# Prompt attention of a hybrid decoder step: queries, keys and values stored by head, weighing on two column halves, sums of probabilities on GpSimd

## The chip, the cores and the metric

The kernel runs on one core of a Trainium2 chip. The metric is the device time of one execution in microseconds; the time before is the median of three runs.

## The reference

One inference step of a two-layer decoder trunk for a prompt of 2048 tokens and eight samples of eight new tokens each, all in fp32. The part that the change touches is the forgetting attention of the prompt in the even layer, with 8 heads of 64:

```python
def fox_prompt(q, k, v, logf):              # blocks of 128 queries
    cum = jnp.cumsum(logf, axis=1)
    s = einsum('bqhd,bkhd->bhqk', qi, k) * D ** -0.5
    s = s + ci[..., None] - cum_t[:, :, None, :]
    s = where(qpos >= kpos, s, NEG_INF)
    p = softmax(s, axis=-1)
    return einsum('bhqk,bkhd->bqhd', p, v)
```

Before it stand a normalisation and the projection `z = u @ w_in`, which yields q, k and v (k and v are outputs of the step too) and the operands of retention. Behind it come retention, a gated output projection, an RG-LRU layer and a last norm. The samples attend to 8192 cached tokens each, in pages of 128.

## The kernel before

The kernel is written in phases, with engines that meet at semaphores. Each phase ends with a barrier of all engines.

`in_proj` runs twice over 17 token tiles of 128 rows (16 of the prompt, one of the samples). Half 0 makes q, k, v of the attention and rq, half 1 the rest. A tile's four groups of 512 columns are three fp32r matmuls for each of 8 slices (lines 125 to 127), evacuated by ScalarE or VectorE into one buffer `z` per group, and stored by SP as rows of 2 KB to `fq`, `fk`, `fv`, `rq` (line 525).

`attention` handles head t of the prompt and, interleaved, batch t of the samples' cached pages. TensorE, VectorE, ScalarE, GpSimd and SP all walk one list of events, made by `merge` from the prompt's list (`fox_events`) and the samples' (`samp_events`); each engine has handlers for the kinds that concern it. `merge` takes from whichever list has spent the smaller share of its planned cost, and puts an event of the other list ahead if a look would follow a look by less than 0.85 of planned cost. So every planned cost moves the order.

The prompt's 16 key tiles and 4 groups of 512 queries give 40 steps a head (4, 8, 12 and 16). At a step:
- a *look* (lines 1633, 1634) writes scores of a later query block to bank `ps_n`; VectorE masks it where it lies on the diagonal and takes its row maximum (line 1461). The next look waits for that maximum.
- a *score* (1651, 1652) writes transposed scores [keys, queries], with the maximum already taken off, to one of two banks `ps_k`; the diagonal is masked on VectorE (1480).
- *exp* (1368): ScalarE writes the probabilities to one of four buffers `prob`. Tiles on the diagonal have only 384, 256 or 128 of the 512 queries.
- a *weigh* (1667), two steps behind: one fp32 matmul with v as stationary operand. v has a 65th column of ones, so that row 64 of `ps_o` collects the sums of probabilities.

After a group's last weigh comes *keep* (ScalarE copies `ps_o` to `o_t`, 1373), and three steps into the next group *out*: four transposes of `o_t` into bank `ps_x` (1674), from which VectorE divides by the sum (1486, 1490). `ps_x` also serves the transposes of the next head's q and k (1684) and the turned maxima (1641), one at a time.

Of the samples, *s_turn* is VectorE's transpose of gathered keys (1512), after which GpSimd gathers the next group of pages (1293); *s_score* (1692, 1698) and *s_weigh* (1724) are fp32 matmuls in tiles of 32 columns of the array, four side by side. SP loads the V pages (1220), and at a head's end the natural q, k and v of the head after next (1230, 1231): 2048 pieces of 256 B for each of the three, out of token-major rows. GpSimd further copies the high parts of q and k (1320, 1322). `retention` has a product in two column halves (2119): `ps_o[half * HD:(half + 1) * HD, a, :]`.

Of the kernel before, what the change touches and what calls it, by code (L numbers as in the profile page):

```python
# [32 lines left out]
P = 128  # L33
D = 1024
# [320 lines left out]
class AttentionTables:  # L355


    def __init__(self, ph, io):
# [6 lines left out]
        self.causal = ph.sb("causal", [P, NS])  # L365
        self.own = ph.sb("own_half", [P, 2, HD])
# [12 lines left out]
    def load(self, sp):  # L379
        for dst, name in [(self.ident, "identity"), (self.mask, "causal_bias"), (self.mask_t, "causal_bias_t")]:  # L380
            sp.dma_start(dst[:, :], self.io[name]).then_inc(self.consts_in, 16)
# [21 lines left out]
def in_proj(nc, io, half):  # L403


    with ExitStack() as ctx:
# [4 lines left out]
        dests = [io["fq"], io["fk"], io["fv"], io["rq"]] if first else [io["rk"], io["rv"], io["g0"], io["g1"]]  # L411
# [3 lines left out]
        GN = 4  # L415

# [69 lines left out]
        def _(sp):  # L486
            for s in u_stored + z_stored:
                sp.sem_inc(s, 16)
            if first:
# [24 lines left out]
            def step(t, i, par):  # L514
# [19 lines left out]
            for g in range(GN):  # L534
                sp.wait_ge(z_stored[g], 16 * (T + 1))
# [13 lines left out]
        def _(act):  # L549
# [16 lines left out]
            def step(t, i, par):  # L566
# [3 lines left out]
                for g in by_act:  # L570
# [5 lines left out]
                    else:  # L576
                        act.wait_ge(z_stored[g], 16 * (t + 1))
# [27 lines left out]
        def _(dve):  # L605
# [35 lines left out]
            def step(t, i, par):  # L641
# [3 lines left out]
                for g in range(GN):  # L645
                    if g == rot:
                        rotary(t, i, par)
                    elif g in gated:
                        dve.wait_ge(*evac[g].at(t))
                        if g == 2:  # L650
                            dve.wait_ge(z_stored[g], 16 * (t + 1))
# [4 lines left out]
                    elif g not in by_act:  # L656
                        dve.wait_ge(*z_done.at(t, g))
                        dve.wait_ge(z_stored[g], 16 * (t + 1))
# [207 lines left out]
def attention(nc, io, tables):  # L866
# [5 lines left out]
    with ExitStack() as ctx:  # L872
# [25 lines left out]
        def fox_events(last):  # L898
# [3 lines left out]
            for s in range(steps + 2):  # L902
# [136 lines left out]
        v = ph.sb("fox_v_one", [P, 2, PT, HD + 1])  # L1039
# [4 lines left out]
        o_t = ph.sb("fox_o_t", [HD + 1, G])  # L1044
# [64 lines left out]
        ones_set = ph.sem("ones_set")  # L1109
# [11 lines left out]
        weighed = ph.count("weighed", steps, 4)  # L1121
        o_copied = ph.count("o_copied", GQ)
# [52 lines left out]

        def x_free(t, u):
# [33 lines left out]
        def _(sp):  # L1210
            sp.sem_inc(stored, 16)
            for n, name in enumerate(["fq", "fk"]):
                sp.dma_start(nat_s[:, n, :], io[name][LAST, 0:ROWS, :]).then_inc(s_consts_in, 16)
# [14 lines left out]
            def fetch(t, par, rows_ready=()):  # L1228
                for n, name in enumerate(["fq", "fk"]):
                    sp.dma_start(nat[:, n], io[name][0:PT, :, bass.ds(t * HD, HD)].rearrange("t p d -> p t d")).then_inc(head_in, 16)  # L1230
                sp.dma_start(v[:, par, :, 0:HD], io["fv"][0:PT, :, bass.ds(t * HD, HD)].rearrange("t p d -> p t d")).then_inc(v_in[par], 16)
# [1929 lines left out]
```

## Time and profile before

| | |
|---|---|
| three runs | 3680.77, 3687.21, 3688.68 us; median 3687.21 |
| profiled execution | 3679.39 us, span 3677.7 |
| busy | TensorE 3280.4, weight loads 2492.7, VectorE 1721.9, ScalarE 1282.1, GpSimd 296.6 |
| mean granted TensorE clock | 0.94 |
| DMA | 360931 packets, 627.36 MB, 118185 of them under 512 B |
| projection, half 0 and half 1 | to about 440, to about 850 us |
| attention | from about 917 to 1976 us |

Times are of one execution, in microseconds from the start of its span. PE is TensorE's matmuls and PEld its weight loads, DVE is VectorE, ACT ScalarE and POOL GpSimd. A matmul's record includes the latency of its tail, so that records overlap; the distance from start to start tells what one costs in a stream. An fp32 matmul leaves two load records and two matmul records; a transpose, and an fp32r matmul, one of each. A shape such as 128*65 gives the rows and columns of the array that an instruction uses.

### The profile page before, as it was taken

The page shows a single profiled execution, that of the slowest core. Times are in us where ns is not written, and L with a number is a line of the kernel's source. Part 1 is how long each engine was busy: PE and PEld are TensorE (multiplying, and loading weights), DVE is VectorE, ACT ScalarE, POOL GpSimd, SP SyncE. Part 2 cuts the span into 40 slices and gives each one's busy share as a digit, 9 for nine tenths or more (in the row PEclk, how much of TensorE's full clock was granted, in tenths as well). Part 3 has the DMA queues.
Part 4 walks back from the last instruction along what each step waited for, and adds up shares of the span by engine and source line. Part 5 has one row for each costly group of instructions (what it writes and reads, how often), then busy time and mean ns, then how long its engine had stood idle before and what let it go on. Part 6 is the DMA issues. An engine that isn't in the chain of part 4 may idle for free. (4 is left out here: it accounts for less than half of the span.)

```text
span 3677.7 us, 63038 instructions
## 1 busy us (share of the span) xinstructions
PE 3280.4 (89%) x22374; PEld 2492.7 (68%) x22374; DVE 1721.9 (47%) x2974; ACT 1282.1 (35%) x2326; POOL 296.6 (8%) x306
## 2 busy tenths in 40 slices
PE   6999789995799899999996859999869999499998
PEld 5888678884465565556554757888747777378887
DVE  3222221242676666667652744333346676443333
ACT  3111121211134334334433533333356666533232
POOL 0000000111211111111100530000000000000000
PEclk9999899996599999999998979999979999699999
DMA  5333442344688888888866863333244433332221
GB/s 140 116 116 115 173 133 96 107 142 124 214 300 285 265 317 281 272 281 312 293 207 204 291 237 121 113 117 127 94 174 138 129 129 109 114 119 91 79 90 59
DMA packets 360931, 627.36 MB, mean 171 GB/s; under 512 B 118185, under 2 KB 180689, under 8 KB 344274
## 3 DMA queue, kind: packets, MB, share of 16 engines
q1 hardware_dynamic: 341410, 487.62, 39.6%
q0 software_dynamic: 19264, 136.46, 10.6%
q8 instruction: 144, 2.36, 0.3%
q14 instruction: 113, 0.93, 0.1%
HBM read 488.74 MB, written 135.22 MB: 170 GB/s over the span
## 5 line engine op out<-in xcount | busy, mean ns | idle before, releaser
L125 PE MATMUL in_ps_z<-in_w_hi,in_u_hi 128*128 128x512 f32 x952 | 375.4, 394 | 41.5 <-DVE in_w_lo L159 41.5
L126 PE MATMUL in_ps_z<-in_w_lo,in_u_hi 128*128 128x512 f32 x952 | 374.3, 393 | 0.0
L127 PE MATMUL in_ps_z<-in_w_hi,in_u_lo 128*128 128x512 f32 x952 | 373.9, 393 | 0.0
L1512 DVE STREAM_TRANSPOSE att_samp_kt<-att_samp_k_ring 128x1024 f32<-128x1024 f32 x256 | 306.9, 1224 | 25.5 <-DMA att_samp_k_ring<-cache_k,att_samp_rows_now 13.2
L1667 PE MATMUL att_fox_ps_o<-att_fox_prob,att_fox_v_one 128*65 128x512 f32 (+3 forms) x640 | 290.4, 537 | 10.1 <-ACT att_fox_prob L1368 9.8
L1368 ACT ACTIVATE att_fox_prob<-att_fox_ps_k 128x512 f32<-128x512 f32 (+1 forms) x320 | 167.6, 531 | 243.6 <-DVE att_fox_ps_k L1480 154.7
L125 PEld LDWEIGHTS in_ps_z<-in_w_hi,in_u_hi 128*128 128x128 f32 x952 | 181.1, 190 | 80.5 <-issue 28.6
L125 PE MATMUL tail_ps_g<-tail_wg_hi,tail_h_hi 128*128 128x512 f32 x544 | 216.3, 398 | 13.6 <-DVE tail_p_lo L2396 9.8
L1461 DVE TENSOR_REDUCE att_fox_part_max<-att_fox_ps_n 128x1 f32<-128x512 f32 (+2 forms) x320 | 193.3, 604 | 75.0 <-PE att_fox_ps_n L1634 65.9
L126 PE MATMUL tail_ps_g<-tail_wg_lo,tail_h_hi 128*128 128x512 f32 x544 | 212.7, 391 | 0.0
L127 PE MATMUL tail_ps_g<-tail_wg_hi,tail_h_lo 128*128 128x512 f32 x544 | 212.6, 391 | 0.0
L127 PEld LDWEIGHTS in_ps_z<-in_w_hi,in_u_lo 128*128 128x128 f32 x952 | 181.0, 190 | 38.3
L126 PEld LDWEIGHTS in_ps_z<-in_w_lo,in_u_hi 128*128 128x128 f32 x952 | 181.0, 190 | 37.1
L1293 POOL DMA_INDIRECT att_samp_k_ring<-cache_k,att_samp_rows_now x128 | 121.3, 947 | 753.0 <-DVE att_samp_kt L1512 684.8
L1651 PE MATMUL att_fox_ps_k<-att_fox_q_a,att_fox_k_a 128*128 128x512 f32 (+1 forms) x320 | 168.0, 525 | 10.9 <-issue 8.6
L2424 DVE SCALAR_TENSOR_TENSOR tail_e<-tail_ps_g,tail_e 128x512 f32<-128x512 f32 x68 | 47.0, 692 | 278.3 <-ACT tail_ps_g L2357 278.3
L1724 PEld LDWEIGHTS att_samp_ps_v<-att_samp_v_ring,att_samp_prob_t 128*16 128x16 f32 x4096 | 102.5, 98 | 75.0 <-issue 63.5
L1698 PE MATMUL att_samp_ps_s<-att_samp_kt,att_samp_q_blocks 128*32 128x128 f32 x4096 | 151.6, 293 | 0.0
L1698 PEld LDWEIGHTS att_samp_ps_s<-att_samp_kt,att_samp_q_blocks 128*32 128x32 f32 x4096 | 112.8, 116 | 51.3 <-issue 48.9
L1724 PE MATMUL att_samp_ps_v<-att_samp_v_ring,att_samp_prob_t 128*16 128x128 f32 x4096 | 140.4, 279 | 5.1 <-DMA att_samp_v_ring<-cache_v 5.0
L1633 PE MATMUL att_fox_ps_n<-att_fox_k_a,att_fox_q_a 128*128 128x512 f32 (+2 forms) x320 | 127.9, 400 | 17.7 <-DVE att_fox_part_max L1461 14.7
L125 PEld LDWEIGHTS tail_ps_g<-tail_wg_hi,tail_h_hi 128*128 128x128 f32 x544 | 102.6, 189 | 47.8 <-DVE tail_h_lo L2417 21.3
(385 smaller groups left out, 6854.6 us busy)
## 6 DMA issues: line engine op xcount, KB each, us to landing
att_samp_v_ring<-cache_v SPq DMA_DIRECT2D x512, 256.0 KB
tail_a_hi<-a_hi SPq DMA_DIRECT2D x34, 512.0 KB, 5.9
tail_a_lo<-a_lo SPq DMA_DIRECT2D x34, 512.0 KB, 6.2
in_w_stage<-w_in_even SPq DMA_DIRECT2D x64, 256.0 KB, 6.6
lru_u_hi<-u_hi SPq DMA_DIRECT2D x8, 2048.0 KB, 8.1
lru_u_lo<-u_lo SPq DMA_DIRECT2D x8, 2048.0 KB, 13.2
in_x<-x SPq DMA_DIRECT2D x17, 512.0 KB, 3.7
u_hi<-in_u_hi SPq DMA_DIRECT2D x17, 512.0 KB, 3.9
```

Source lines behind the costliest of these rows:

```text
L125: pe.matmul(out, act_hi, w_hi, start=start, stop=False)
L126: pe.matmul(out, act_hi, w_lo, start=False, stop=False)
L127: return pe.matmul(out, act_lo, w_hi, start=False, stop=stop)
L1293: pool.indirect_dma_start(k_ring[:, n % KR, :], None, io["cache_k"], bass.IndirectOffsetOnAxis(ap=rows_now[:, par, n:n + 1], axis=0)).then ...
L1368: act.activation(prob[:, s % 4, r:G], ps_k[:, s % 2, r:G], ACT.Exp).then_inc(exped.sem, 1)
L1461: dve.tensor_reduce(part_max[:, g, b % B4, c:c + 1], ps_n[:, 0:w], AX.X, ALU.max).then_inc(maxed.sem, 1)
L1512: ins = dve.transpose(kt[:, n % 2, :, :].rearrange("p c (s i) -> p s c i", s=SLOTS)[:, p * two:(p + 1) * two], k_ring[:, n % KR, p * two * ...
L1633: pe.matmul(ps_n[:, 0:w], q_a[:, par, q], k_a[:, par, k], start=True, stop=False)
L1651: pe.matmul(ps_k[:, s % 2, r:G], k_a[:, par, k], q_a[:, par, q], start=True, stop=False)
L1667: pe.matmul(ps_o[0:HD + 1, r:G], v[:, par, kt, :], prob[:, s % 4, r:G], start=kt == 0, stop=kt == B4 * (g + 1) - 1).then_inc(weighed.sem, 1)
L1698: last = pe.matmul(ps_s[h * QUAD:(h + 1) * QUAD, at:at + PAGE], q_blk[:, bpar, block, :], kt[:, y, block, :], start=False, stop=y == 1 and ...
L1724: last = pe.matmul(acc[a * QUAD:a * QUAD + 2 * NS, :], prob_t[:, c % 2, at:at + 2 * NS], v_ring[:, y, p, a * P:(a + 1) * P], start=c == 0 ...
```

## The change

Half 0 of the projection stores q, k and v by head, in scratch tensors [head, partition, token tile, 64], in pieces of 256 B; k and v go to `fk` and `fv` as well, q no longer to `fq`. Attention loads a head's q, k and v in 128 pieces of 4 KB each.

Weighing goes by pairs of key tiles, at odd steps only: the even tile of a pair writes partitions 0 to 63 of `ps_o`, the odd one 64 to 127. v loses its column of ones. GpSimd adds up the probability tiles of a group in one of two buffers `prob_sum`; ScalarE's exp waits for that addition as well as for the weigh before it reuses a buffer. *Out* becomes four matmuls with `o_t` [128, 128] stationary and a table (two stacked identities of 64) moving, which turn it and add the halves, and four with `prob_sum` stationary and a column of ones moving. The planned cost of a pair is 0.5 of its two widths, before it was 0.87 of each.

```diff
+        by_head = {0: io["hq"], 1: io["hk"], 2: io["hv"]} if first else {}
+        copies = [1, 2, 2, 1] if first else [1] * GN
...
                 for g in range(GN):
                     sp.wait_ge(*kept(g, t))
-                    sp.dma_start(row(dests[g], t), z[:, g, :]).then_inc(z_stored[g], 16)
+                    if g in by_head:
+                        sp.dma_start(by_head[g][:, :, bass.ds(t, 1), :].rearrange("h p o d -> p h (o d)"),
+                                     z[:, g, :].rearrange("p (h d) -> p h d", h=H)).then_inc(z_stored[g], 16)
+                    if dests[g] is not None:
+                        sp.dma_start(row(dests[g], t), z[:, g, :]).then_inc(z_stored[g], 16)
...
-                if s >= 2:
+                if s % 2 and s >= 3:
                     g, kt = group_of(s - 2)
-                    out.append((0.87 * cut_width(kt - B4 * g), ("weigh", g, s - 2, kt)))
+                    out.append((0.5 * (cut_width(kt - 1 - B4 * g) + cut_width(kt - B4 * g)), ("weigh", g, s - 3, kt - 1), ("weigh", g, s - 2, kt)))
...
-        v = ph.sb("fox_v_one", [P, 2, PT, HD + 1])
+        v = ph.sb("fox_v", [P, 2, PT, HD])
+        prob_sum = ph.sb("fox_prob_sum", [P, 2, G])
...
             def fetch(t, par, rows_ready=()):
-                for n, name in enumerate(["fq", "fk"]):
-                    sp.dma_start(nat[:, n], io[name][0:PT, :, bass.ds(t * HD, HD)].rearrange("t p d -> p t d")).then_inc(head_in, 16)
-                sp.dma_start(v[:, par, :, 0:HD], io["fv"][0:PT, :, bass.ds(t * HD, HD)].rearrange("t p d -> p t d")).then_inc(v_in[par], 16)
+                for n, name in enumerate(["hq", "hk"]):
+                    sp.dma_start(nat[:, n], io[name][bass.ds(t, 1), :, 0:PT, :].rearrange("o p t d -> (o p) t d")).then_inc(head_in, 16)
+                sp.dma_start(v[:, par, :, :], io["hv"][bass.ds(t, 1), :, 0:PT, :].rearrange("o p t d -> (o p) t d")).then_inc(v_in[par], 16)
...
+            def add(t, i, par, g, s, kt):
+                nonlocal newest
+
+                if kt == 0:
+                    return
+                r, out = max(kt - B4 * g, 0) * P, prob_sum[:, g % 2, :]
+                pool.wait_ge(*exped.at(t, s))
+                if kt == 1:
+                    pool.wait_ge(*(o_turned.at(t, g - 2) if g >= 2 else o_turned.at(t - 1, g - 2 + GQ)))
+                    pool.wait_ge(*newest)
+                    if r:
+                        pool.sem_inc(pool_passed, 1)
+                        pool.tensor_copy(out[:, 0:r], prob[:, (s - 1) % 4, 0:r]).then_inc(first_added.sem, 1)
+                        pool.wait_ge(*first_added.at(t))
+                    ins = pool.tensor_tensor(out[:, r:G], prob[:, (s - 1) % 4, r:G], prob[:, s % 4, r:G], ALU.add)
+                else:
+                    pool.wait_ge(*added.at(t, s - (g + 1) - 1))
+                    pool.wait_ge(*newest)
+                    ins = pool.tensor_tensor(out[:, r:G], out[:, r:G], prob[:, s % 4, r:G], ALU.add)
+                ins.then_inc(added.sem, 1)
+                newest = added.at(t, s - (g + 1))
...
                 act.wait_ge(*(weighed.at(t, s - 4) if s >= 4 else weighed.at(t - 1, s - 4 + steps)))
+                act.wait_ge(*added_at(t if s >= 4 else t - 1, s - 4))
...
-                act.copy(o_t[:, :], ps_o[0:HD + 1, :]).then_inc(o_copied.sem, 1)
+                act.copy(o_t[:, :], ps_o[:, :]).then_inc(o_copied.sem, 1)
...
-                pe.matmul(ps_o[0:HD + 1, r:G], v[:, par, kt, :], prob[:, s % 4, r:G],
-                          start=kt == 0, stop=kt == B4 * (g + 1) - 1).then_inc(weighed.sem, 1)
+                half = slice(kt % 2 * HD, kt % 2 * HD + HD)
+                pe.matmul(ps_o[half, r:G], v[:, par, kt, :], prob[:, s % 4, r:G],
+                          start=kt < 2, stop=kt >= B4 * (g + 1) - 2, skip_group_check=True).then_inc(weighed.sem, 1)
...
                 for b in range(B4):
-                    last = pe.transpose(ps_x[:, b * P:b * P + HD + 1], o_t[:, b * P:(b + 1) * P], ident[0:HD + 1, 0:HD + 1])
+                    halves = HD if g == 0 and b == 0 else P
+                    pe.matmul(ps_x[:, b * P:b * P + HD], o_t[0:halves, b * P:(b + 1) * P], tables.fold[0:halves, 0:HD], start=True, stop=True)
+                pe.wait_ge(*added.at(t, sum(B4 * (x + 1) - 1 for x in range(g + 1)) - 1))
+                for b in range(B4):
+                    last = pe.matmul(ps_x[:, b * P + HD:b * P + HD + 1], prob_sum[:, g % 2, b * P:(b + 1) * P], tables.fold[:, HD:HD + 1],
+                                     start=True, stop=True)
```

Besides, the table `fold` is loaded with the other tables, `ps_o` is zeroed once by VectorE in place of the ones, the samples' q rows come from `hq`, and GpSimd's copies wait for its newest result.

## Rows read from the trace of the kernel before

**Rows 1.** Windows: two stages; busy us and count by engine, clock, DMA.

```profile
core 0: us, PE busy (x) PEld busy (x) DVE busy (x) ACT busy (x) POOL busy (x), PEclk, DMA share, GB/s
60.00:440.00 380.00, 371.77 (x2064) 324.62 (x2062) 91.24 (x179) 51.56 (x92) 0.00 (x0) 1.00 0.31 116
...
1013.00:1976.00 963.00, 905.18 (x10613) 564.77 (x10613) 615.44 (x1118) 375.23 (x860) 143.07 (x178) 0.98 0.82 277
```

**Rows 2.** Waits of PE in 1013 to 1976: us in total, times, longest.

```profile
PE att_fox_ps_o L1667 <- ACT att_fox_prob L1368: 9.8, 7, 1.4
PE att_fox_ps_k L1651 <- issue: 8.6, 2, 5.2
PE att_fox_ps_x L1684 <- DVEq L1493: 6.6, 7, 1.0
...
PE att_samp_ps_v L1724 <- DMA att_samp_v_ring<-cache_v: 5.0, 5, 2.5
```

**Rows 3.** Groups by form, 1013 to 1977: busy us, mean ns, idle before.

```profile
L1512 DVE STREAM_TRANSPOSE att_samp_kt<-att_samp_k_ring 128x1024 f32<-128x1024 f32 x222 | 265.8, 1224 | 11.4 <-issue 7.3 <-DVE att_fox_out L1490 2.4 <-DVE att_fox_k_b L1501 1.6
...
L1293 POOL DMA_INDIRECT att_samp_k_ring<-cache_k,att_samp_rows_now x110 | 104.2, 947 | 697.0 <-DVE att_samp_kt L1512 638.9 <-ACT att_fox_q_a L1379 43.6 <-issue 14.6
```

**Rows 4.** Timeline of PE at 1308: start, us, line, output and inputs.

```profile
1307.76 0.50 PE L1651 MATMUL att_fox_ps_k<-att_fox_q_a,att_fox_k_a 128*128 128x512 f32 x1
1308.10 0.40 PE L1652 MATMUL att_fox_ps_k<-att_fox_q_b,att_fox_k_b 98*128 98x512 f32 x1
1308.33 0.40 PE L1633 MATMUL att_fox_ps_n<-att_fox_k_a,att_fox_q_a 128*128 128x512 f32 x1
1308.57 0.40 PE L1634 MATMUL att_fox_ps_n<-att_fox_k_b,att_fox_q_b 96*128 96x512 f32 x1
1308.81 1.02 PE L1667 MATMUL att_fox_ps_o<-att_fox_prob,att_fox_v_one 128*65 128x512 f32 x2
1309.76 1.07 PE L1724 MATMUL att_samp_ps_v<-att_samp_v_ring,att_samp_prob_t 128*16 128x128 f32 x32
1310.76 0.46 PE L1674 MATMUL att_fox_ps_x<-att_tables_ident,att_fox_o_t 65*128 65x65 f32 x4
```

**Rows 5.** Timeline of PE in retention, at 2084.

```profile
2084.74 1.09 PE L2119 MATMUL ret_ps_o<-ret_scores,ret_qkv 128*64 128x128 f32 x16
2085.77 1.09 PE L2143 MATMUL ret_ps_a<-ret_ident,ret_gated 128*128 128x128 f32 x8
...
2087.59 1.06 PE L2127 MATMUL ret_ps_u<-ret_qkv,ret_k_decayed 128*128 128x128 f32 x8
2088.48 0.27 PE L2095 MATMUL ret_ps_q<-ret_ident,ret_qkv 128*128 128x128 f32 x1
```

**Rows 6.** Timeline of weight loads: L1766 at 1245, L1674 at 1310.

```profile
1245.73 0.41 PEld L1766 LDWEIGHTS att_samp_ps_t<-att_samp_totals,att_tables_sum_rows 128*128 128x128 f32 x3 [0.24 <-issue]
...
1310.76 0.33 PEld L1674 LDWEIGHTS att_fox_ps_x<-att_tables_ident,att_fox_o_t 65*128 65x128 f32 x4 [0.21 <-DVEq L1503]
```

**Rows 7.** Timeline at a head's end: a look, its maximum, the samples' chain.

```profile
1124.03 0.39 PE L1634 MATMUL att_fox_ps_n<-att_fox_k_b,att_fox_q_b 96*128 96x512 f32 x1
...
1124.26 1.02 PE L1667 MATMUL att_fox_ps_o<-att_fox_prob,att_fox_v_one 128*65 128x512 f32 x2
...
1124.45 0.69 DVE L1461 TENSOR_REDUCE att_fox_part_max<-att_fox_ps_n 128x1 f32<-128x512 f32 x1 [0.20 <-PE att_fox_ps_n L1634]
...
1125.82 0.19 PE L1781 MATMUL att_samp_ps_t<-att_tables_ident,att_samp_neg_most 2*128 2x2 f32 x1 [0.54 <-DVE att_samp_inv L1578]
```

**Rows 8.** Group on POOL in retention: an fp32 operation with two SBUF inputs.

```profile
L1942 POOL TENSOR_TENSOR ret_state<-ret_state,ret_state_table 128x512 f32<-128x512 f32 x16 | 20.4, 1274 | 7.8 <-PE ret_ps_o L2119 7.8
```

**Rows 9.** DMA issues by line: KB each, median us to landing.

```profile
att_fox_natural<-fq SPq DMA_DIRECT2D x8, 512.0 KB, 4.0
...
att_fox_v_one<-fv SPq DMA_DIRECT2D x8, 512.0 KB, 6.7
fo<-att_fox_out SPq DMA_DIRECT2D x8, 512.0 KB, 4.5
```

More of the change, by code:

```diff
@@ L365, in __init__ @@
         self.causal = ph.sb("causal", [P, NS])
+        self.fold = ph.sb("fold", [P, HD + 1])
         self.own = ph.sb("own_half", [P, 2, HD])
@@ L379, in load @@
     def load(self, sp):
-        for dst, name in [(self.ident, "identity"), (self.mask, "causal_bias"), (self.mask_t, "causal_bias_t")]:
+        for dst, name in [(self.ident, "identity"), (self.mask, "causal_bias"), (self.mask_t, "causal_bias_t"), (self.fold, "fold")]:
             sp.dma_start(dst[:, :], self.io[name]).then_inc(self.consts_in, 16)
@@ L410, in in_proj @@
         w_in = io["w_in_even"][0].rearrange("(k p) n -> p k n", p=P)
-        dests = [io["fq"], io["fk"], io["fv"], io["rq"]] if first else [io["rk"], io["rv"], io["g0"], io["g1"]]
+        dests = [None, io["fk"], io["fv"], io["rq"]] if first else [io["rk"], io["rv"], io["g0"], io["g1"]]
         rot = 3 if first else 0
@@ L486, in _ @@
         def _(sp):
-            for s in u_stored + z_stored:
+            for s in u_stored:
                 sp.sem_inc(s, 16)
+            for g in range(GN):
+                sp.sem_inc(z_stored[g], 16 * copies[g])
             if first:
@@ L534, in _ @@
             for g in range(GN):
-                sp.wait_ge(z_stored[g], 16 * (T + 1))
+                sp.wait_ge(z_stored[g], 16 * copies[g] * (T + 1))
             if first:
@@ L1121, in attention @@
         weighed = ph.count("weighed", steps, 4)
+        added = ph.count("added", steps - GQ)
+        first_added = ph.count("first_added")
         o_copied = ph.count("o_copied", GQ)
@@ L1174, in attention, with added_at @@
         out_kept = ph.count("s_out_kept")
+        def added_at(t, s):
+            s = s if s >= 0 else s + steps
+            g, kt = group_of(s)
+            return added.at(t, s - (g + 1) + (kt == 0))
         def x_free(t, u):
@@ L1288, in _ @@
         def _(pool):
-            lead(pool, doubled, rows_kept)
+            lead(pool, doubled, rows_kept, added, first_added)
+            newest = None
             def gather(b, par, n):
@@ L1317, in turn @@
                 pool.wait_ge(*(doubled.at(t, j - 1) if j else doubled.at(t - 1)))
+                nonlocal newest
+                if newest is not None:
+                    pool.wait_ge(*newest)
+                newest = doubled.at(t, j)
                 pool.sem_inc(pool_passed, 1)
@@ L1328, in s_exp_new @@
                     pool.wait_ge(*k_turned.at(t))
+                    nonlocal newest
+                    pool.wait_ge(*newest)
+                    newest = rows_kept.at(t + 2)
+                    pool.sem_inc(pool_passed, 1)
                     pool.tensor_copy(rows_now[:, par, :], tables.rows[:, bass.ds((t + 2) * NKG, NKG)]).then_inc(rows_kept.sem, 1)
@@ L1339, in _, with head @@
             pool.wait_ge(tables.samp_in, 6 * 16)
-            one, step = run({"turn": turn, "s_turn": s_turn, "s_exp_new": s_exp_new})
+            one, step = run({"turn": turn, "exp": add, "s_turn": s_turn, "s_exp_new": s_exp_new})
             one(-1, -1, 1, opening)
-            each_tile(pool, step, H, peel=2)
+            def head(t, i, par):
+                nonlocal newest
+                pool.wait_ge(*doubled.at(t))
+                newest = added.at(t - 1)
+                step(t, i, par)
+            each_tile(pool, head, H, peel=2)
         @block.scalar
@@ L1432, in _ @@
                  k_turned, s_maxed, new_biased, new_maxed, s_topped, most_made, neg_made, negated, new_kept, totalled, closing, out_kept)
-            dve.memset(v[:, :, :, HD:HD + 1], 1.0).then_inc(ones_set, 1)
             set_rows(dve, 0, rows_set)
             dve.memset(ps_v[:, :], 0.0)
+            dve.memset(ps_o[:, :], 0.0)
             dve.memset(q_blk[:, :, :, :], 0.0).then_inc(bd_zeroed, 1)
@@ L3060, in tables @@
     c["causal_bias_t"] = c["causal_bias"].T
+    c["fold"] = np.concatenate([np.tile(np.eye(HD), (2, 1)), np.ones((P, 1))], axis=1)
     page = page_order(n_pages)
```

23 lines of the change are left out of this document (12 added, 11 removed).

## Prediction

> **What bounds the kernel now.** I read the stages first [rows 1]. In the prompt's input projection (60 to 440) TensorE is busy 98% of the time at the full clock with DMA at 0.31: a store there hides as long as it keeps up. The changed attention runs from about 917 to 1976; its regular part, 1013 to 1976, is 963 us with TensorE busy 905, a granted clock of 0.98 (so nearly always the upper of its two levels, 2.4 GHz), VectorE 615, ScalarE 375, GpSimd 143, DMA 0.82. Next I asked what TensorE waited for [rows 2]. All its idle time there is 58 us, in short waits that come back once a head; waits for the maxima (VectorE) of looks and for cache pages hardly occur. So the stage is bound by what TensorE must stream, and a microsecond of streaming removed is worth one until another engine becomes late. VectorE is next: 64% busy, and each look waits for the maximum of the look before it.
>
> A busy time of TensorE holds the tail of each record, so I price streaming by starts [rows 4]. A full-width weighing (L1667) starts at 1308.81 and its successor at 1309.76: 0.95 us, of which about 0.86 is its own (two passes of 0.43) and 0.09 the change to 32-column tiles that follows.
>
> **The weighing.** A head weighs 40 key tiles: 28 full-width and four each of 384, 256 and 128 queries, 34 full widths in all, 34 x 0.86 = 29.2 us. The change runs them as 20 pairs, one in each column half. If both halves stream together a pair costs its wider member: 12 + 4 full pairs and 4 of 256 make 18 widths, 15.5 us. That they do is shown by retention's L2119 [rows 5]: eight matmuls in alternating column halves, 16 passes of 128 columns, take 1.03 us, 0.064 a pass, where L2127 with all columns needs 0.89 for 8, 0.111 a pass. Gain: 13.7 x 8 = 110 us.
>
> The halves are another mode of the array. L2119's 1.03 us is 0.17 over its eight rounds of 0.107; entry adds 0.09 [rows 4]; behind a tiled burst the first load is bare (L1651 to L1652 takes 0.34 where later pairs take 0.23). So an excursion from full mode and back is some 0.36 us. From the planner's rule the order comes out so: per head 33 excursions now, 36 afterwards (many pairs land beside a sample burst, which has paid for one side), and 16 crossings between halves and quarters. A crossing stands in no row; between nothing and a whole excursion I take 0.15, a drain and a short load. Cost: 3 x 0.36 + 16 x 0.15 = 3.5 us a head, 28 us; with free crossings 9, with whole ones 55. The weighing then gives 82 us (55 to 101).
>
> **The turn back.** Four transposes per group become four matmuls against the fold table and four of one column on the sums. An fp32 matmul leaves two load and two matmul records, so 16 of each stand for 4. Their length is that of loading 128 stationary columns. L1766 is just such a product with one moving column: three loads start to end in 0.41 us, each 0.19, so 0.11 apart; the transposes of L1674 load every 0.063 us ((0.33 - 0.14) / 3) [rows 6]. I take 0.11, since type, shape and moving column are L1766's: 16 x 0.11 - 4 x 0.063 = 1.5 us, 32 times: 49 us given back. At 0.063 it would be 24 us. The Trainium skill (TensorE: Matmul & The Clock Gate, LDWEIGHTS) puts a load at columns divided by 1.2 ns, estimated 107 ns here, for both forms alike; then the extra would be 12 loads, 1.28 us or 41 us in all, 8 less. L1766 agrees with it, L1674 does not, and I go by the rows.
>
> **Looks closer together.** Now a weighing of 0.86 us stands in every gap between looks; afterwards in every second. A look's maximum is ready 0.42 + 0.69 us after the start of its second matmul [rows 7]; with the wake-up of TensorE, some 0.1, and 0.23 of own streaming taken off, 0.98 us of other work must lie in the gap. The planner moves a sample event into most of them (0.46 score + 1.0 burst is enough). By its rule three gaps a head are left with 0.12, 0.35 and 0.46 us, since K transposes are no work for TensorE and diagonal scores are narrow: 0.86 + 0.63 + 0.52 = 2.0 us. At the head's end the weighing at 1124.26 covers part of the sample's chain up to L1781 [rows 7]; it moves behind, so up to 0.86 more is waited. Together 2.8 us a head, 22 us. Below it could be 0 if neighbouring waits absorb them; above, if all 20 bare gaps lost the 0.52 of a lone score, 83 us.
>
> **GpSimd.** 36 additions a head, 24 of them full: a full-width fp32 tensor_tensor takes 1.27 us [rows 8], narrower ones in proportion, about 39 us of a head's 120. It does 18 now. It has room, and four probability buffers leave an addition three steps. Queued behind the additions are the gathers of K pages (L1293), which now sit 639 us waiting for VectorE [rows 3] and leave as soon as it is done. In the planner's order an addition of step s starts after the exponential and ends about when VectorE, having taken the look's maximum and two transposes of 1.2 us [rows 3], releases the gather: 0 to 1.3 us of lag on 110 gathers, of which most land early. I take 3 us (0 to 20). The matmuls of the sums wait for the last addition three steps old: nothing; at the head's end it runs beside the last weighing and its copy.
>
> **By-head layout.** Each token tile issues three stores of 1024 pieces of 256 B, one in place of a plain one, on SP. The same size of piece is stored by L1275 (fo), 512 KB landing in 4.5 us [rows 9]; so at most three times that against a tile of some 22 us (380 / 17), in a stage whose queue is a third full; TensorE is not stopped while the buffers are free within a tile. What can show is the last tile's stores before the phase closes: 1 us. Without the cover, if they landed after the next tile's evacuation, the price would be the excess times 17. In attention the three loads of a head go from 2048 pieces to 128, which spares the queues; they land 4 to 7 us after issue [rows 9] and are wanted tens of microseconds later, so only the 5 us of page waits [rows 2] could shrink: 3 us of gain. The first loads, the table and a memset of ps_o in place of the ones: +1.
>
> **Sum.** -82 + 49 + 22 + 3 + 1 + 1 - 3 = -9, say -10 us. The profiled execution took 3679.39 (span 3677.7 and 1.7 around), which would become 3669. It is 7.8 below the median of the runs shown, 3687.21, so against that 3677. Within 0.2%, 7.4 us, this measurement can't tell a change from none; the forecast lies just outside.
>
> **Rivals.**
> - Cheap turn: loads 0.063 apart and crossings almost free: -82 - 15 + 24 + 22 + 2 = -49, 3638; only one of both, about -33, 3654. For it: L1674. Against: L1766.
> - Slower, because the looks starve: the point is where the bare gaps together lose 32 us instead of 22 (0.2 us on each of 160). At 0.45 us on 110 of them, 50 us, it is +18, 3705. For it: VectorE at 64% and K transposes of 1.2 us each in front of its maxima. Against: today no look waits, and a burst stands in most gaps.
> - The halves do not overlap wholly. If the second tile's first pass starts only with the first tile's second, a pair takes three passes, 1.30 us, not 0.86: 18 x 0.43 x 8 = 62 us back, +52, 3739. For it: the weighing's passes are four times longer than L2119's, and each carries a semaphore. Against: with one unshared pass of 0.107 for each matmul, L2119's eight would need 0.96 us after the first pass and L1724's sixteen 1.8, where 1.03 with its drain and 1.00 stand [rows 4, 5]; L1724 decides. The Trainium skill (TensorE: Matmul & The Clock Gate, What overlaps and what doesn't) says that loads overlap running matmuls only where the row group differs, and matmuls start and end in order; column halves share their row group. The trace speaks against it.
> - Gathers lag: if a third of 110 is late by 1 us the gain is gone, +27 at most with V pages late too, 3710. For it: DMA at 0.82. Against: GpSimd half idle.
> - The layout does nothing and the weighing cancels with the turn: within 7 us, 3684.
>
> **Chances.** Forecast 0.45 (own range 3660 to 3692; two thirds of it faster, a quarter same), cheap turn 0.17, looks starve 0.20, no overlap 0.06, gathers 0.04, nothing 0.08. Faster 0.30 + 0.17 + 0.02 = 0.49; same 0.11 + 0.08 + 0.02 = 0.21; slower 0.30. Likeliest 3677; holding 8 in 10 from the cheap turn to the starved looks: 3645 to 3712.
>
> **What would show it.** Right: weighing records of the two halves starting a few ns apart, a pair about 0.9 us; two starts of turn loads 0.11 apart and the turn 1.7 to 1.8 us; 963 us shrinking by about 10; three waits a head for the look's maximum; GpSimd at some 450 us with unchanged K waits; the projection's 380 us unchanged. Wrong: halves 0.43 us apart; K or V waits over 20 us; TensorE's idle time in attention above 58 + 40 us; a projection that grew.

## The result, and the profile after

The changed kernel takes 3743.69 us (median of four runs, 3737.45 to 3757.6) against 3684.69 us for the kernel before beside it (3680.77 to 3688.68). The medians lie 59 us apart; the measured ratio is 1.0169, with a 95% interval of 1.0152 to 1.0187, which is 62 us, and that figure is used from here on. The forecast was 3677 in a range of 3645 to 3712, so side and range are both wrong.

The windows of the changed kernel, for the same two stages as [rows 1]:

```profile
core 0: us, PE busy (x) PEld busy (x) DVE busy (x) ACT busy (x) POOL busy (x), PEclk, DMA share, GB/s
60.00:440.00 380.00, 372.23 (x2067) 325.06 (x2065) 91.37 (x179) 51.56 (x92) 0.00 (x0) 1.00 0.44 140
1022.00:2033.00 1011.00, 912.17 (x10982) 579.36 (x10982) 642.77 (x1117) 376.19 (x859) 460.17 (x472) 0.95 0.77 264
```

The projection is what it was, with DMA at 0.44 instead of 0.31: the stores by head hide. Attention's regular part went from 963 to 1011 us, 48 of the 58 us by which this pair of executions differs (spans 3677.7 and 3735.8); 9 of the others lie ahead of the first weighing, which starts at 1022.9 instead of 1013.8. What brings those was not found: with the layout alone it is 3 us. Two things in the row are new. TensorE has 99 us of idle time instead of 58, and its granted clock is 0.95 instead of 0.98. Summed over the clock's own records, time at the lower level (1.2 GHz) between the first and the last weighing of that part went from 38 to 109 us. What TensorE does at the lower level takes nearly twice as long: a burst of 32 records of L1786, from start to start, 1.84 us there and 1.00 at the upper level. Of the time at the lower level TensorE was busy for 30 us before and for 99 after, and about half of that is lost: 15 and 50 us, 35 more. Idle time (41 more) and clock make 76 us, and they outweigh everything that the edits save.

TensorE's waits there, to be held against [rows 2] (us in total, times, longest):

```profile
PE att_fox_ps_n L1689 <- DVE att_fox_part_max L1518: 25.0, 46, 1.0
PE att_fox_ps_x L1746 <- DVEq L1560: 13.4, 14, 1.3
PE att_samp_ps_v L1786 <- DMA att_samp_v_ring<-cache_v: 12.6, 8, 3.5
PE att_samp_ps_t L1843 <- DVE att_samp_inv L1635: 11.6, 7, 1.8
PE att_fox_ps_x L1746 <- DVEq L1550: 6.2, 7, 0.9
```

First the looks, which hardly waited before; then the turning bank, `ps_x`; then a V page; then the sample's chain at the end of a head. The priced streams, however, came out about as priced. The timeline of TensorE at a pair (start, us, idle before):

```profile
1319.53 0.51 PE L1689 MATMUL att_fox_ps_n<-att_fox_k_a,att_fox_q_a 128*128 128x512 f32 x1 [0.64 <-DVE att_fox_part_max L1518]
1319.87 0.40 PE L1690 MATMUL att_fox_ps_n<-att_fox_k_b,att_fox_q_b 96*128 96x512 f32 x1
1320.20 1.07 PE L1724 MATMUL att_fox_ps_o<-att_fox_prob,att_fox_v 128*64 128x512 f32 x4
1321.20 1.07 PE L1786 MATMUL att_samp_ps_v<-att_samp_v_ring,att_samp_prob_t 128*16 128x128 f32 x32
```

The four records of L1724 are two weighings of two passes, here a pair on the diagonal, 512 and 384 queries wide. A pair of full width takes as long:

```profile
1034.44 1.08 PE L1724 MATMUL att_fox_ps_o<-att_fox_prob,att_fox_v 128*64 128x512 f32 x4
1035.45 1.07 PE L1786 MATMUL att_samp_ps_v<-att_samp_v_ring,att_samp_prob_t 128*16 128x128 f32 x32
```

Two passes of one weighing took 1.02 before [rows 4]. The two halves stream side by side. Added up from start to start, waits behind it included, weighing went from 253 to 171 us, 82 less. The turn back, in its weight loads:

```profile
1306.03 1.11 PEld L1732 LDWEIGHTS att_fox_ps_x<-att_tables_fold,att_fox_o_t 64*128 64x128 f32 x8 [0.21 <-issue]
1307.06 0.97 PEld L1735 LDWEIGHTS att_fox_ps_x<-att_tables_fold,att_fox_prob_sum 128*128 128x128 f32 x8
```

Eight loads on the sums in 0.97 us, each 0.19, are (0.97 - 0.19) / 7 = 0.11 us apart, as L1766's [rows 6]. GpSimd's additions cost what L1942's row gave [rows 8], and the gathers waited only 316 us instead of 697 [rows 3], 260 of it still for VectorE, hence early:

```profile
L1366 POOL TENSOR_TENSOR att_fox_prob_sum<-att_fox_prob_sum,att_fox_prob 128x512 f32<-128x512 f32 x168 | 214.7, 1278 | 92.5 <-ACT att_fox_prob L1425 81.3 <-POOL att_fox_prob_sum L1366 2.3 <-POOL att_fox_q_b L1343 1.2
L1312 POOL DMA_INDIRECT att_samp_k_ring<-cache_k,att_samp_rows_now x109 | 104.8, 961 | 315.9 <-DVE att_samp_kt L1569 260.4 <-ACT att_fox_prob L1425 48.6 <-issue 4.8
```

What does a starved look look like? Ahead of the one above the timeline of the engines reads:

```profile
1317.44 1.08 PE L1760 MATMUL att_samp_ps_s<-att_samp_kt,att_samp_q_blocks 128*32 128x128 f32 x32
1317.46 1.23 DVE L1569 STREAM_TRANSPOSE att_samp_kt<-att_samp_k_ring 128x1024 f32<-128x1024 f32 x1
1318.45 0.33 PE L1707 MATMUL att_fox_ps_k<-att_fox_q_a,att_fox_k_a 128*128 128x128 f32 x1
1318.61 0.28 PE L1708 MATMUL att_fox_ps_k<-att_fox_q_b,att_fox_k_b 98*128 98x128 f32 x1
1318.62 0.27 DVE L1537 TENSOR_TENSOR att_fox_ps_k<-att_fox_ps_k,att_tables_mask_t 128x128 f32<-128x128 f32 x1
1318.80 0.67 DVE L1518 TENSOR_REDUCE att_fox_part_max<-att_fox_ps_n 128x1 f32<-128x512 f32 x1
```

TensorE has a sample burst and a narrow score between two looks, no weighing. VectorE has a K transpose and a mask of the score ahead of the maximum, which ends at 1319.47; the next look starts at 1319.53. Of the 45 such waits between the first and the last weighing, 38 have no weighing in their gap. In 26, which hold 14 of 24 us, a K transpose stands in the unbroken run of VectorE's work ahead of the maximum, in the others masks alone.

### The profile page after: what moved, and what is told of

Same layout as the page of the kernel before. It is cut to its first block and busy times, and to the rows that moved or that the text cites. A ratio compares the mean times of both kernels' runs of the same rounds, so it can differ in the third digit from the quotient of the medians.

```text
span 3735.8 us, 65259 instructions
## 1 busy us (share of the span) xinstructions
PE 3290.1 (88%) x22758; PEld 2511.1 (67%) x22758; DVE 1747.7 (47%) x2974; ACT 1282.8 (34%) x2326; POOL 614.4 (16%) x602
## 5 line engine op out<-in xcount | busy, mean ns | idle before, releaser
L1366 POOL TENSOR_TENSOR att_fox_prob_sum<-att_fox_prob_sum,att_fox_prob 128x512 f32<-128x512 f32 (+3 forms) x256 | 276.7, 1081 | 157.1 <-ACT att_fox_prob L1425 139.3
L1724 PE MATMUL att_fox_ps_o<-att_fox_prob,att_fox_v 128*64 128x512 f32 (+3 forms) x640 | 166.3, 571 | 2.3 <-ACT att_fox_prob L1425 2.3
L1707 PE MATMUL att_fox_ps_k<-att_fox_q_a,att_fox_k_a 128*128 128x512 f32 (+1 forms) x320 | 151.3, 473 | 8.2 <-ACT att_fox_prob L1425 4.6
L608 POOL TENSOR_TENSOR in_z<-in_gate_silu,in_gn 128x512 f32<-128x512 f32 x17 | 25.1, 1478 | 799.3 <-DVE in_gate_silu L663 799.3
L1786 PE MATMUL att_samp_ps_v<-att_samp_v_ring,att_samp_prob_t 128*16 128x128 f32 x4096 | 142.4, 282 | 15.9 <-DMA att_samp_v_ring<-cache_v 12.6
L1786 PEld LDWEIGHTS att_samp_ps_v<-att_samp_v_ring,att_samp_prob_t 128*16 128x16 f32 x4096 | 103.4, 99 | 74.5 <-issue 52.0
```

Source lines behind the costliest of these rows:

```text
L1366: ins = pool.tensor_tensor(out[:, r:G], out[:, r:G], prob[:, s % 4, r:G], ALU.add)
L1707: pe.matmul(ps_k[:, s % 2, r:G], k_a[:, par, k], q_a[:, par, q], start=True, stop=False)
L1724: pe.matmul(ps_o[half, r:G], v[:, par, kt, :], prob[:, s % 4, r:G], start=kt < 2, stop=kt >= B4 * (g + 1) - 2, skip_group_check=True).then ...
L1786: last = pe.matmul(acc[a * QUAD:a * QUAD + 2 * NS, :], prob_t[:, c % 2, at:at + 2 * NS], v_ring[:, y, p, a * P:(a + 1) * P], start=c == 0 ...
```

## Experiments

Each ratio is to the kernel before, run on the same chip; a per cent is 37 us. "Idle" and "lower clock" are TensorE's, in us, between the first and the last weighing of the regular part: 58 and 38 before, 98 and 109 after. They come from one profiled execution of each kernel, which lies up to 9 us beside the median of its kernel, and 15 to 25 for the three orders with the new spacing rule.

**The order alone** (in the kernel before):

```
-                if s >= 2:
+                if s % 2 and s >= 3:
                     g, kt = group_of(s - 2)
-                    out.append((0.87 * cut_width(kt - B4 * g), ("weigh", g, s - 2, kt)))
+                    out.append((0.5 * (cut_width(kt - 1 - B4 * g) + cut_width(kt - B4 * g)), ("weigh", g, s - 3, kt - 1), ("weigh", g, s - 2, kt)))
```

> The kernel before with one edit: the weighings come in pairs in every second gap, in the order and with the planner's costs of the changed kernel. Each weighing still streams all columns, one after the other, and the layout, the ones column and the turn back are those of before. Theory A (the order starves the looks, and TensorE's clock falls behind the waits): the trace of the changed kernel has 41 us more idle TensorE and 72 us more at the lower clock, 36 us lost, so this kernel takes 40 to 77 us more than before, 3725 to 3762 us. Rival B (the order is harmless while a pair of full weighings takes 1.7 us; it is the shorter pair that leaves looks bare): 0 to 20 us more, 3685 to 3705. Rival C (the stalls come from the sums on GpSimd or the turn back): no change, 3685 within 7.

Measured: 3736.98 us, ratio 1.0139 (1.0121 to 1.0158), 51 us. Idle 97, lower clock 72. Its waits are those of the changed kernel:

```profile
PE att_fox_ps_n L1633 <- DVE att_fox_part_max L1461: 21.8, 41, 0.9
PE att_fox_ps_x L1684 <- DVEq L1503: 14.0, 14, 1.3
PE att_samp_ps_v L1724 <- DMA att_samp_v_ring<-cache_v: 11.1, 6, 4.2
PE att_samp_ps_t L1781 <- DVE att_samp_inv L1578: 10.1, 7, 1.6
```

Theory A holds for the idle time: no instruction differs, only the order, and the 39 us more are there. The clock is another matter. The time at the lower level rises by 34 us in this profile; over all executions, what the clock takes away (one less the mean granted clock, times the span) is 228 us here, 221 before and 266 in the changed kernel. So the order alone brings the waits and little of the clock's part. That a full pair is longer does not help, so rival B falls. The edit changes two things at once, the pairing and the planned cost; which of them spoils the order is not told apart here.

**The layout alone** (the stores and loads by head in the kernel before).

> The kernel before with the by-head stores and loads alone. All theories that put the loss into attention's order expect 3685 us within 7: the stages ahead of attention were 6 us longer in the changed kernel, the head loads might give back 3. A rival, that the stores by head or the loads disturb memory traffic and through it TensorE's clock, expects 3695 to 3710.

Measured: 3684.53 us, ratio 1.0005 (0.9995 to 1.0015). The layout neither costs nor gives anything that can be told. Idle 57, lower clock 48: with the order of before the latter is 10 us more than in the profile before, which shows how far one execution can stray.

**No sums on GpSimd.** From the changed kernel:

```
-            one, step = run({"turn": turn, "exp": add, "s_turn": s_turn, "s_exp_new": s_exp_new})
+            one, step = run({"turn": turn, "s_turn": s_turn, "s_exp_new": s_exp_new})
...
-                act.wait_ge(*added_at(t if s >= 4 else t - 1, s - 4))
```

> The changed kernel with the additions on GpSimd left out, and every wait on them; the sums are set to a constant once, so the denominators are not the reference's. The matmuls that turn back are as before. Theory A (order): ScalarE waits for the additions nowhere that decides, so 3736 to 3744 us. Rival C (late additions hold the probability buffers and delay exponentials, scores and the turn back): 20 to 40 us less, 3704 to 3724.

Measured: 3747.61 us, ratio 1.0164 (1.0145 to 1.0184), the changed kernel's within the intervals. GpSimd's 320 us of additions hide wholly. Idle 103, lower clock 130.

**Both weighings in one half** (from the changed kernel):

```
-                half = slice(kt % 2 * HD, kt % 2 * HD + HD)
+                half = slice(0, HD)
```

> The changed kernel with both weighings of a pair in the same column half, so that they can't stream side by side; everything else as it is. If the halves overlap as the starts in the trace show, each pair takes 0.86 us more at full width, 13.7 us a head, 110 us in all; under theory A the longer pair covers some of the waits for looks and gives back 20 to 40 of it: 3815 to 3850 us. If the halves did not overlap and this were the cause of the loss, 3744 us within 10.

Measured: 3825.77 us, ratio 1.0393 (1.0371 to 1.0416), 82 us above the changed kernel. The four records of the full pair now take

```profile
1034.45 1.93 PE L1724 MATMUL att_fox_ps_o<-att_fox_prob,att_fox_v 128*64 128x512 f32 x4
1036.31 1.07 PE L1786 MATMUL att_samp_ps_v<-att_samp_v_ring,att_samp_prob_t 128*16 128x128 f32 x32
```

1.86 us from start to start instead of 1.01: two passes of 0.43 more. Weighing as a whole takes 270 us instead of 171. So the halves overlap, and 82 of the 100 us arrive. The missing 18 can be seen: idle 86, lower clock 89, so the kernel with overlap has 13 us more idle time and 20 us more at the lower clock.

**64 columns instead of 65** (the order alone, and the tile mode):

```
-                pe.matmul(ps_o[0:HD + 1, r:G], v[:, par, kt, :], prob[:, s % 4, r:G],
+                pe.matmul(ps_o[0:HD, r:G], v[:, par, kt, 0:HD], prob[:, s % 4, r:G],
```

> The kernel before with the changed order, and each weighing on 64 columns of the array instead of 65 (in one half, one after the other, so nothing overlaps and nothing is saved in streaming). The ones column is left out, so the denominators are not the reference's. It prices what the tile mode alone costs beside the order. My term for the switches of mode was 28 us (9 to 55). What is left when the order, the turn and the layout are taken from the run with both weighings in one half is 46 us: that theory (switches dearer than I took) expects 41 to 55 us above the run of the order alone (ratio 1.0139), 3732 + 46 = 3778 against 3681 of before. If 28 is right: 3760. If the tile mode costs nothing: 3732.

Measured: 3759.36 us, ratio 1.0215 (1.0198 to 1.0232). Above the order alone that is 0.76%, 28 us, give or take 9: my term for the changes of mode, and not the 46 of the other theory. Idle 95, lower clock 55.

**The turn back of before** (from the changed kernel):

```
-                    pe.matmul(ps_x[:, b * P:b * P + HD], o_t[0:halves, b * P:(b + 1) * P], tables.fold[0:halves, 0:HD], start=True, stop=True)
+                    last = pe.transpose(ps_x[:, b * P:b * P + HD + 1], o_t[0:HD + 1, b * P:(b + 1) * P], ident[0:HD + 1, 0:HD + 1])
...
-                for b in range(B4):
-                    last = pe.matmul(ps_x[:, b * P + HD:b * P + HD + 1], prob_sum[:, g % 2, b * P:(b + 1) * P], tables.fold[:, HD:HD + 1],
-                                     start=True, stop=True)
```

> The changed kernel with the turn back of before: four transposes of 65 rows for each group, no fold of the odd half and no matmul on the sums (both are left out, so the attention output is not the reference's; the reciprocal reads another column). The additions on GpSimd stay. If the turn is priced right (49 us by loads 0.11 us apart; 47 in the trace of the changed kernel, start to start), this takes 3697 us, and up to 10 more where the turn covered a wait: 3690 to 3710. If the turn's loads hide in waits that are there anyway (a theory in which TensorE waits for VectorE most of the time and streams for nothing), 3735 to 3744.

Measured: 3701.85 us, ratio 1.0053 (1.0036 to 1.0070). The turn costs 1.16%, 43 us. Idle 116, lower clock 137: without the turn TensorE waits 17 us more.

**The looks spaced by the planner** (from the changed kernel):

```
-                    since[k] = 0.0 if k in kinds(e) else since[k] + e[0]
+                    since[k] = 0.0 if k in kinds(e) else since[k] + (0.0 if "s_turn" in kinds(e) else e[0])
...
-        SPACE = 0.85
+        SPACE = 1.0
-        TURN = 8
+        TURN = 12
```

> The changed kernel with three numbers of the planner changed: a K transpose, which is no work for TensorE, counts nothing towards the space between two looks, the space asked for is 1.0 instead of 0.85, and the turning of the next head's queries and keys starts at step 12 instead of 8. No instruction is added or removed. Theory A (the order made bare gaps, and the waits pull the clock down): TensorE's idle time falls from 98 us to 50 to 70, time at the lower clock from 109 to 40 to 70 us, so 3744 - 38 - 27 = 3679, range 3665 to 3705. Rival B (a short pair leaves too little work in the gaps, wherever it is put): 3730 to 3744.

Measured: 3752.67 us, ratio 1.0201 (1.0183 to 1.0218): no gain, where 3679 was expected. Idle 90, lower clock 120. The waits for maxima nearly went, and others came:

```profile
PE att_samp_ps_s L1754 <- ACT att_samp_scores L1451: 25.3, 28, 1.4
PE att_samp_ps_v L1786 <- DMA att_samp_v_ring<-cache_v: 19.3, 9, 5.6
...
PE att_fox_ps_n L1689 <- DVE att_fox_part_max L1518: 6.5, 21, 0.4
```

The rule spaces looks by pulling sample events forward. These then stand close to each other and wait for their own bank and their own pages. My theory in its narrow form, that the bare gaps of looks are the loss, fell here.

**A balanced order.** The weighings stay in pairs, but the list goes by two steps (in short):

```
+            for s in range(0, steps + 2, 2):
+                    for x in range(2):
+                        out.append((0.46 * cut_width(kt - B4 * g), ("score", g, s + x, kt)))
+                for x in range(2):
+                    if x and s >= 2:
+                        out.append((0.95 * cut_width(kt - 1 - B4 * g), ("weigh", g, s - 2, kt - 1), ("weigh", g, s - 1, kt)))
...
+                            out.append((0.46, ("look", dt, ng, b, c, n)))
...
+        SPACE = 1.7
+        TURN = 10
```

together with the spacing edit above.

> The changed kernel with another order: two scores, a look, the pair of weighings, a look, so that one gap between looks holds 0.92 us of scores and the next 0.95 us of weighing; the space is 1.7 with K transposes counting nothing, turning starts at step 10. Theory A: every gap holds nearly what a look's maximum needs, idle time 40 to 60 us, lower clock 30 to 60 us: 3744 - 48 - 32 = 3664, range 3650 to 3690. Rival B: 3730 to 3744. A second rival, that scores in twos starve of exponentials (both score banks are then taken at once): 3700 to 3720 with new waits for ScalarE.

Measured: 3815.29 us, ratio 1.0362 (1.0345 to 1.0379), a miss by 150 us. Idle 144, lower clock 208. The looks no longer wait (4.5 us), but the crowded sample events do:

```profile
PE att_samp_ps_v L1786 <- DMA att_samp_v_ring<-cache_v: 73.3, 28, 6.6
PE att_samp_ps_s L1754 <- ACT att_samp_scores L1451: 19.3, 22, 1.3
```

**Sums turned by transposes** (the balanced order with turning from step 6; the sums turned in an event of their own):

```
+                for b in range(B4):
+                    last = pe.transpose(ps_x[:, b * P:(b + 1) * P], prob_sum[:, g % 2, b * P:(b + 1) * P], ident[:, :])
...
+                    last = act.activation(sum_dump[:, b, :], ps_x[:, b * P:(b + 1) * P], ACT.Copy, accum_out=sum_q[:, g % 2, b:b + 1])
```

> As the balanced order (turning from step 6), and the sums turned back by four transposes of 128 columns (one load each, 0.063 us apart in the kernel before) in an event of their own instead of eight loads 0.11 us apart; ScalarE adds them up by its accumulator, four operations for each group. On TensorE 0.6 us less for each of 32 groups, 20 us: 3645 if nothing else changes. Rival: the transposes take a fifth turn of the one bank that queries, keys, maxima and outputs are turned in, and its waits (20 us in the changed kernel) eat the gain: 3665 to 3680.

Measured: 3873.56 us, ratio 1.0514 (1.0495 to 1.0534). That is 229 us above what was expected. Idle 182, lower clock 249. It stands on the bad order, and another fill of `ps_x` came on top; whether the transposes would pay in a good order stays open.

**Later turns** (from the changed kernel: `TURN = 14`, `SPACE = 0.6`, a pair counted as 0.9 instead of 0.5 for each width).

> The changed kernel, its order altered by three numbers of the planner: turning of the next head's queries and keys from step 14 instead of 8, a pair of weighings counted as 1.8 us of work, space 0.6 instead of 0.85. The turns then fill gaps in which a look stood bare, and the sample's events stay spread, unlike in the run whose sample events were crowded. Theory D (the loss of the order is waits of all kinds, and they trade against each other: looks against cache pages and sample scores): waits for looks fall without waits for pages growing, 30 to 50 us less than the changed kernel, 3690 to 3715 for a before of 3681. If there is nothing to be had from order: 3735 to 3745.

Measured: 3752.89 us, ratio 1.0206 (1.0189 to 1.0223): no gain, where 3690 to 3715 was expected. Idle 93, lower clock 161. Turned this late, K is not ready when the next head's first look wants it:

```profile
PE att_fox_ps_n L1689 <- POOL att_fox_k_a L1345: 24.3, 7, 3.5
PE att_samp_ps_v L1786 <- DMA att_samp_v_ring<-cache_v: 18.0, 14, 4.1
PE att_fox_ps_n L1689 <- DVE att_fox_part_max L1518: 14.6, 37, 0.6
```

**The balanced order with the old spacing rule** (`SPACE = 0.85`, K transposes counted, `TURN = 11`).

> The order of two scores, a look, a pair of weighings, a look, but with the planner's spacing rule left as it was (space 0.85, K transposes counted) and turning from step 11. Of the earlier balanced run, what cost was the crowding of sample events (73 us of waits for V pages): under theory D it goes away, and with it the starved gaps: 40 to 60 us less than the changed kernel, 3680 to 3705. If the balanced order itself is bad (scores two together wait for exponentials): 3750 and more, with waits for ScalarE.

Measured: 3674.00 us, ratio 0.9981 (0.9968 to 0.9994), 6 us below the expected range. It is 1.9% faster than the changed kernel with the same instructions, and 0.2% faster than the kernel before. Its window and its longest waits:

```profile
1018.00:1968.00 950.00, 897.78 (x10982) 576.60 (x10982) 628.02 (x1117) 372.86 (x858) 460.57 (x471) 0.96 0.82 281
```

```profile
PE att_fox_ps_x L1697 <- DVE att_fox_neg_top L1530: 8.0, 13, 1.4
PE att_fox_ps_n L1689 <- DVE att_fox_part_max L1518: 7.6, 16, 1.8
PE att_samp_ps_v L1786 <- DMA att_samp_v_ring<-cache_v: 7.3, 6, 3.0
PE att_fox_ps_k L1707 <- ACT att_fox_prob L1425: 6.7, 9, 0.8
```

The count of instructions is the changed kernel's (10982 matmul records). Idle time fell to 52 us and the time at the lower clock to 69.

**The balanced order in the kernel before.** Its weighings follow each other over all columns; everything else is as before.

> The kernel before with the balanced order: two scores, a look, the weighings of two steps one after the other over all columns, a look; turning from step 11; nothing else. If the 51 us of the changed order alone were its bare gaps (a gap with a lone score in every second place), they vanish here although the weighings still come in twos: ratio to before 0.995 to 1.003, idle TensorE about 58 us. If weighings in twos cost by themselves (probability buffers, late exponentials), it stays slower, 1.008 or more. It also says what the balanced order with pairs side by side gained from order and what from overlap: with 28 for the mode, 43 for the turn and 82 for the overlap, the changed kernel's own parts are worth 11 us in an order that costs nothing.

Measured: 3673.77 us, ratio 0.9967 (0.9953 to 0.9981). Idle 49, lower clock 44.

```profile
1012.00:1973.00 961.00, 912.20 (x10611) 572.46 (x10610) 607.82 (x1117) 370.63 (x858) 141.95 (x177) 0.98 0.83 277
```

So weighings in twos cost nothing by themselves; the changed kernel's order of them does. (The balanced order alters four things together, the scores in twos, the place of the looks, the planned costs and the step of turning; what each does was not run.) And nothing here is gained by the other edits: pairs side by side in the same order (0.9981) are no faster than this.

## Why the prediction was wrong

The time between the first and the last weighing can be split in three: what TensorE would be busy at the full clock (its busy time, less half of the busy time at the lower level, an estimate), what it is idle, and what the lower clock costs (that half). From the traces, in us:

| kernel | part | busy at full clock | idle | clock |
|---|---|---|---|---|
| before | 963 | 890 | 58 | 15 |
| the order alone | 1022 | 895 | 97 | 30 |
| 64 columns instead of 65 | 1040 | 922 | 95 | 23 |
| both weighings in one half | 1095 | 968 | 86 | 41 |
| changed | 1010 | 862 | 98 | 50 |
| changed, turn back of before | 987 | 812 | 116 | 59 |
| before, balanced order | 961 | 894 | 49 | 18 |
| changed, balanced order | 950 | 866 | 52 | 31 |

**The streaming, -110.** The mechanism was right and the size nearly: TensorE is busy 106 us less with overlap than without, of which 82 arrive in the time of this order. The rival without overlap, whose 3739 lies nearest to the result, is refuted: its time was met by chance. What the Trainium skill (TensorE: Matmul & The Clock Gate, What overlaps and what doesn't) says, weighed in that rival, is that loads overlap running matmuls only where the row group differs. Two column halves share their row group and run together here, four full passes in 1.01 us from start to start.

**The changes of mode, +28.** Measured 28 by the run, 27 by busy time, beside full-width weighings in the same order.

**The turn back, +49.** Measured 43 by the run, 50 by busy time. The loads lie 0.11 us apart, as the row of L1766 said. The 41 us by the load rule of the Trainium skill (TensorE: Matmul & The Clock Gate, LDWEIGHTS) can't be told from 49 by the run, whose interval is some 9 us to either side; the busy time speaks for 49. The rival of a cheap turn, 24, is out.

**GpSimd +3, layout and first loads +2, shorter loads -3.** Measured: 0 within the intervals for the sums, 2 for the layout with an interval that holds zero; the 5 us of page waits were not reduced but grew to 13.

**Looks closer together, +22.** This is the step that failed. The order alone costs 51, 39 of them idle time. I summed three bare gaps a head that the planner's rule left, and took the other gaps as covered, since a sample burst or score stood in them. The trace has 46 waits of 0.54 us, six a head. In more than half of them VectorE has a K transpose of 1.2 us ahead of the maximum, which I had put under the starving rival, so my 0.98 us of needed cover was too small. Beyond the looks, the step left out what the same order does elsewhere: waits for `ps_x` (from 8 to 20 us), for V pages (from 5 to 13) and for the sample's chain at the end of a head (from 4 to 12). My own sign of being wrong, idle time above 58 + 40, was just met with 98.5.

**What had no term at all: the clock.** I read 0.98 and kept it. Its part goes from 15 to 50 us in the regular part. The order alone brings 7 us of that over its executions, 15 in its profile; the rest comes with the rest of the change, and what brings it stays open (below). The rival of starved looks (+18 against before, 3705) had the right mechanism for the looks but neither the other waits nor the clock.

By the table the regular part grew by -28 + 41 + 35 = 48 us. The -28 stands for my -110 + 28 + 49 = -33: what I priced as streaming came out. Idle time and clock, 76 us, stand for my 22. The runs say the same less closely: 51 (order) + 28 (mode) + 43 (turn) + 2 (layout) - 82 (overlap) = 42, where 62 was measured, since each took waits and clock along from another base. The 20 us between show up between the kernel with both weighings in one half and the one with 64 columns, which differ by 66 us where turn and layout explain 45: the clock takes 18 more in the first, idle time 9 less, and 8 lie ahead of the first weighing.

In the balanced orders the rest of the change makes 0.9981 - 0.9967 = 0.0014, 5 us, with overlapping intervals. TensorE is busy 27 us less there, near the 33, but the clock takes 13 more in the profiles (69 us against 44 at the lower level), and 6 more lie ahead of the first weighing. So even without the spoiled order the change did not bring what its streaming saves.

Two sums of the rivals are slightly off, without bearing on the result: with crossings alone almost free the saving would be about -24, not -33, and +27 for late gathers gives 3714, not 3710.

## What to carry to other kernels

- When an edit moves work between engines, price the new order as a part of its own, by a kernel that has the old instructions in the new order. Here that one part was 51 of 62 us. The work between two looks must be even, rather than enough on average.
- A spacing rule that pulls another stream forward starves that stream. Waits for one resource fell from 25 to 6.5 us here and the time stayed. Judge an order by TensorE's idle time in all, never by one wait.
- Halving the streaming of a product is worth less than it looks if results must be joined afterwards: of 106 us, 27 went to array modes and 50 to the joining, before any order was spoiled.
- Split the time of each run into busy at full clock, idle and clock before adding up terms. A time alone mixes them: leaving out the turn saved 50 us of work and 43 us of time.

## What the hardware showed that I had not expected

- TensorE's clock follows its waits in jumps. In the changed kernel, after a wait of 1.7 us for the sample's chain at the end of a head and 2 us of idle time within 16, the clock was at the lower level for the whole of the next 20 us, though TensorE was busy for 17 of them:

```profile
1255.00:1271.00 16.00, 13.97 (x180) 8.04 (x172) 10.37 (x23) 3.82 (x7) 10.64 (x10) 0.98 0.84 296
1271.00:1291.00 20.00, 17.35 (x112) 11.67 (x112) 6.93 (x18) 7.35 (x23) 1.77 (x4) 0.50 0.41 113
1291.00:1311.00 20.00, 18.27 (x225) 11.60 (x224) 12.41 (x24) 6.40 (x15) 8.71 (x10) 1.00 0.79 274
```

- The time at the lower clock does not follow from idle time alone. The order alone and the changed kernel have the same idle time (97 and 98 us) but 72 and 109 us at the lower clock. Runs with 49, 52 and 58 us idle have 44, 69 and 38. Nor is less streaming the cause: with both weighings in one half TensorE is busy 46 us more than with 64 columns and idle 9 us less, and yet spends 89 us at the lower clock against 55. No edit taken out alone gives the clock back. Over all executions it takes 266 us in the changed kernel, 265 without the sums, 257 with the turn of before and 257 with both weighings in one half, against 228 for the order alone, 225 for the layout alone and 221 before. Why was not found.
- Two fp32 products in two column halves stream together even at 512 columns a pass: four passes in 1.01 us from start to start, against 1.86 in one half.
